# Raw-stream routers, and the experts' gather and sums as fp32r products of a rounded high part and a rest, in a two-block network on one Trainium2 core

## What is computed

```python
def rms_norm(x, g):
    xf = x.astype(F32)
    y = xf * lax.rsqrt(jnp.mean(xf * xf, axis=-1, keepdims=True) + EPS)
    return (y * g.astype(F32)).astype(x.dtype)

# per layer i:   hn = rms_norm(h, norm_ffn[i]);  h = h + hier_moe(hn, ...)
def hier_moe(h, wr_g, br_g, wr_e, br_e, w_gu, w_down):
    xf = h.reshape(T, D)
    p_group = softmax(xf @ wr_g + br_g)                 # 4 groups, top 1
    e_logits = xf @ wr_e + br_e                         # 32 experts, top 2 of the 8 in the group
    gates = pg * pv / jnp.sum(pv, axis=-1, keepdims=True)
    return grouped_experts(xf, expert_id, gates, w_gu, w_down)
# one expert on its tokens xb:  a, b = split(xb @ w_gu[e]);  (silu(a) * b) @ w_down[e]
# the rows are weighted by their gate and summed back to their tokens
```

## Time and profile before

| | |
|---|---|
| median of the runs | 2223.04 us |
| the profiled execution's own time | 2214.99 us |
| its span, first to last instruction | 2213.1 us |
| mean granted TensorE clock | 0.982 |
| busy: PE, DVE, ACT | 2089.7, 892.3, 669.1 us |
| HBM read | 600.73 MB |
| loop over the pairs, layer 0 | 951.2 to 1430.3 us |
| loop over the pairs, layer 1 | 1712.0 to 2189.3 us |

### The profile page before, as it was taken

One profiled execution on the slowest core, in us unless ns is written; L12 is line 12 of the kernel. 1 busy time (PEld: TensorE's weight loads), 2 busy tenths in 40 slices (PEclk: granted clock), 3 DMA queues, 4 the chain that ended last, 5 costly groups with the idle time before them and its releaser, 6 DMA issues.

```text
span 2213.1 us, 38037 instructions
## 1 busy us (share of the span) xinstructions
PE 2089.7 (94%) x15784; PEld 1525.4 (69%) x15785; DVE 892.3 (40%) x1468; ACT 669.1 (30%) x958; POOL 79.6 (4%) x118
## 2 busy tenths in 40 slices
PE   7997899998999998989999999999998999999998
PEld 5876899988999897844454444588987444444444
DVE  5866678745643544521111111165275111111112
ACT  3434464253652466311111111144342011111111
POOL 0100111101000200000000000000000000000000
PEclk9998999999999999999999999999999999999999
DMA  9731389803655251779999999535631899999993
GB/s 361 262 129 48 139 306 333 317 31 115 228 176 187 77 191 41 288 287 421 422 422 422 422 422 422 226 115 190 247 148 77 356 419 422 422 422 422 422 422 126
DMA packets 108084, 603.26 MB, mean 273 GB/s; under 512 B 10062, under 2 KB 10500, under 8 KB 58836
## 3 DMA queue, kind: packets, MB, share of 16 engines
q1 hardware_dynamic: 95872, 559.39, 63.9%
q0 software_dynamic: 11840, 42.34, 5.3%
q10 hardware_dynamic: 276, 0.13, 0.0%
HBM read 600.73 MB, written 1.05 MB: 272 GB/s over the span
## 4 chain that ended last, share of the span: by engine, by line
PE 88%; DVE 4%; ACT 4%; issue 2%; DMA 2%; SPq 0%; DVEq 0%; ACTq 0%
PE bank L939 20%; PE bank L951 10%; PE bank L551 10%; PE bank L552 10%; PE bank L553 10%; PE bank L923 6%; PE bank L970 5%; PE bank L581 4%; DMA dense_w<-in_w_in 1%; PE bank L561 1%; PE bank L562 1%; PE bank L560 1%; PE bank L594 1%; PE bank L631 1%; DVE work L1514 1%
## 5 line engine op out<-in xcount | busy, mean ns | idle before, releaser
L939 PE MATMUL bank<-expert_w,work 128*32 128x512 f32 (+1 forms) x4032 | 447.7, 594 | 24.0 <-issue 21.5
L939 PEld LDWEIGHTS bank<-expert_w,work 128*32 128x32 f32 (+1 forms) x4032 | 156.1, 110 | 314.2 <-issue 314.2
L434 DVE TENSOR_TENSOR w_low<-dense_w,w_high 128x2048 fp32r<-128x2048 f32 x112 | 256.1, 2290 | 221.5 <-ACT w_high L427 220.8
L427 ACT ACTIVATE w_high<-dense_w 128x2048 fp32r<-128x2048 f32 x120 | 228.6, 1911 | 312.1 <-DMA dense_w<-in_mlp_w 195.1
L951 PE MATMUL bank<-expert_w,work 128*32 128x512 f32 (+1 forms) x2016 | 226.4, 594 | 0.0
L2075 DVE TENSOR_TENSOR work<-work,bank 128x512 f32<-128x512 f32 x32 | 22.0, 688 | 400.3 <-ACT work L1404 400.3
L951 PEld LDWEIGHTS bank<-expert_w,work 128*32 128x32 f32 (+1 forms) x2016 | 63.5, 110 | 144.5 <-issue 144.5
L923 PEld LDWEIGHTS bank<-work 128*128 128x128 f32 x1088 | 133.1, 199 | 33.9 <-issue 33.8
L551 PE MATMUL bank<-u_pairs_mlp,w_high 128*128 128x256 f32 x512 | 145.2, 284 | 6.0 <-ACT u_pairs_mlp L1140 6.0
L923 PE MATMUL bank<-work 128*128 128x128 f32 x1088 | 139.2, 287 | 6.9 <-issue 6.9
L551 PE MATMUL bank<-hidden_pairs,w_high 128*128 128x256 f32 x512 | 144.9, 283 | 0.0
(11 more groups left out here) (379 smaller groups left out, 3620.8 us busy)
## 6 DMA issues: line engine op xcount, KB each, us to landing
expert_w<-in_expert_w_gu SPq DMA_DIRECT2D x256, 1024.0 KB, 13.1
expert_w<-in_expert_w_down SPq DMA_DIRECT2D x128, 1024.0 KB, 9.6
dense_w<-in_mlp_w SPq DMA_DIRECT2D x64, 1024.0 KB, 5.5
dense_w<-in_ret_w_in SPq DMA_DIRECT2D x24, 1024.0 KB, 5.4
u<-in_ada_w POOLq DMA_DIRECT2D x40, 512.0 KB, 6.2
work<-in_ada_w POOLq DMA_DIRECT2D x40, 512.0 KB, 6.9
dense_w<-in_fox_w_in SPq DMA_DIRECT2D x16, 1024.0 KB, 5.0
dense_w<-in_w_in SPq DMA_DIRECT2D x12, 1024.0 KB, 8.1
```

The lines of the kernel that those rows point to most:

```text
L427: nc.scalar.activation(HIGH_OF[at], dense_w[:, at % RING], ACT.Copy, scale=scale).then_inc(S("w_high_ready"), 1)
L434: ins = nc.vector.tensor_tensor(w_low[:, at % RING], dense_w[:, at % RING], high, ALU.subtract)
L939: last = mm(free[half][cols, :], rows[:, k, cols], pieces[:, k // 2, a, k % 2, half * 512:(half + 1) * 512], start=k == 0, stop=k == KT - 1)
```

## The change

- `moe_norm` goes. PE turns the raw `h` (4 banks of 4 transposes), and the router multiplies raw `h` by router weights that were scaled once by the norm's gain (a DVE product over both layers, ahead of the fox projections). The logits are multiplied by the token's reciprocal deviation when DVE reads them. ACT gets the squares' sums from the turned banks, and their root.
- The normed tokens are kept as `hn_high` (rounded, ACT) and `hn_low` (the rest, DVE), without the gain, which is applied when `xg` is copied. `pick` becomes fp32r. The gather is two fp32r products in place of each f32 one.
- y is kept as `y_high` and `y_low`; the slot's weight `slot_w`, summed from the turned `pick_w`, is applied at that copy, and `pickT` is zeros and ones. `add_up` is two fp32r products in place of each f32 one. The two halves of y are now each made by ACT and then by DVE.
- The eight warming products ahead of the first gather go, the order of `take_h` and of the weighing of the first pick is moved, and a fifth late load brings the gain, two values of each layout row in one run.

```diff
-                   ("moe_norm_0", 1), ("router_0", 2), ("hn_0", 4), ("combine_0", 4),
+                   ("hn_0", 4), ("router_0", 2), ("combine_0", 4),
...
+        hn_high = parts("hn_high", "work", 0, [TT, D])
+        hn_low = parts("hn_low", "u", 0, [TT, D])
...
+        y_high = parts("y_high", "work", 5632, [D])
+        y_low = parts("y_low", "work", 9728, [D])
+        pick = parts("pick", "work", 6656, [TT, P])
...
+        pickT = parts("pickT", "work", 7680, [TT * P])
+        slot_w = small[:, 92:93]
...
             def experts(l):
-                rms_norm(f"moe_norm_{l}")
+                out = TILES["ret_out" if l else "fox_out"]
+                for q in range(4):
+                    t = TILES[f"hn_{l}"] + q
+                    tt, half = q % 2, q // 2
+                    open_bank(pe, t)
+                    for n in range(4):
+                        k = 4 * half + n
+                        wait_evac(pe, out + k)
+                        last = nc.tensor.transpose(bank(t)[:, n * P:(n + 1) * P], h[:, k, tt * P:(tt + 1) * P], ident)
+                    last.then_inc(tile_ready, 1)
...
-                        last = mm(bank(t)[:, tt * NR:(tt + 1) * NR], u[:, k, tt * P:(tt + 1) * P], router_w[:, l, k, :],
+                        last = mm(bank(t)[:, tt * NR:(tt + 1) * NR], h[:, k, tt * P:(tt + 1) * P], router_w[:, l, k, :],
...
+                take_h(0)
+                take_h(1)
...
+                take_h(2)
+                take_h(3)
...
                         for tt in range(TT):
-                            last = mm(free[2 + half][:, (k % 4) * P:(k % 4 + 1) * P], every_other(hn_tok[:, tt], k),
-                                      source[:, tt, :], start=tt == 0, stop=tt == TT - 1)
+                            for x in (hn_high, hn_low):
+                                last = mm(free[2 + half][:, (k % 4) * P:(k % 4 + 1) * P], every_other(x[:, tt], k), source[:, tt, :],
+                                          start=tt == 0 and x is hn_high, stop=tt == TT - 1 and x is hn_low)
...
                     for k in range(KT):
-                        last = mm(total[k // 2][:, (k % 2) * SEQ:(k % 2 + 1) * SEQ], y_sb[:, k * P:(k + 1) * P],
-                                  pick_wT.rearrange("p t n -> p (t n)"), start=False, stop=False)
+                        for y in (y_high, y_low):
+                            last = mm(total[k // 2][:, (k % 2) * SEQ:(k % 2 + 1) * SEQ], y[:, k * P:(k + 1) * P], pickT,
+                                      start=False, stop=False)
...
-                for _ in range(WARM):
-                    mm(free[3][:, 0:SEQ], ident, K("rope_cos"), start=True, stop=True)
...
             def experts(l):
-                rms_squares(f"moe_norm_{l}", added("ret_out" if l else "fox_out"))
+                eps = const[:, CONSTS["eps"][0]:CONSTS["eps"][0] + 1]
+                fn(small[:, 90:91], eps, ACT.Sqrt)
+                for q in range(4):
+                    wait_tile(act, TILES[f"hn_{l}"] + q)
+                    at = 80 + 2 * (q // 2) + q % 2
+                    fn(part(wk, 4096 + 512 * q, 512), bank(TILES[f"hn_{l}"] + q)[:, :], ACT.Square,
+                       accum_out=small[:, at:at + 1]).then_inc(S("hn_moments"), 1)
+                act.wait_ge(S("hn_stats"), 2 * l + 1)
+                fn(small[:, 86:88], small[:, 84:86], ACT.Sqrt, scale=1.0 / D, bias=eps).then_inc(S("hn_moments"), 1)
+                act.wait_ge(S("hn_stats"), 2 * l + 2)
+                for q in range(4):
+                    fn(hn_high[:, q % 2, q // 2 * 512:(q // 2 + 1) * 512], bank(TILES[f"hn_{l}"] + q)[:, :], ACT.Copy,
+                       scale=small[:, 88 + q % 2:89 + q % 2]).then_inc(S("hn_high"), 1)
...
                 def take_xg(rows, done):
-                    fn(rows[:, 0:4, :], free[2][:, :].rearrange("p (k n) -> p k n", k=4), ACT.Copy).then_inc(done, 1)
+                    for k in range(4):
+                        last = fn(rows[:, k, :], free[2][:, k * P:(k + 1) * P], ACT.Copy, scale=ffn_gain[:, KT * l + k:KT * l + k + 1])
+                    last.then_inc(done, 1)
...
                 def take_y(done):
-                    fn(y_sb[:, 0:512], free[2][:, :], ACT.Copy).then_inc(done, 1)
+                    for half in range(2):
+                        fn(y_high[:, half * 512:(half + 1) * 512], free[2 + half][:, :], ACT.Copy, scale=slot_w).then_inc(done, 1)
...
+            ffn_rows = vec[:, P + VEC2["ffn"]:P + VEC2["ffn"] + DEPTH * KT].unsqueeze(2).broadcast_to([P, DEPTH * KT, NR])
+            routers = router_w[:, :, :, :].rearrange("p l k n -> p (l k) n")
+            V.tensor_tensor(routers, routers, ffn_rows, ALU.mult).then_inc(S("cum_ready"), 1)
...
+                dve.wait_ge(S("hn_moments"), 5 * l + 4)
+                V.tensor_tensor(small[:, 84:86], small[:, 80:82], small[:, 82:84], ALU.add).then_inc(S("hn_stats"), 1)
+                V.tensor_scalar(y_low, const[:, 0:D], 0.0, None, ALU.mult).then_inc(S("y_dve"), 1)
+                V.tensor_scalar(pickT, const[:, 0:SEQ], 0.0, None, ALU.mult).then_inc(S("pick_wT_ready"), 1)
+                dve.wait_ge(S("hn_moments"), 5 * l + 5)
+                V.reciprocal(small[:, 88:90], small[:, 86:88]).then_inc(S("hn_stats"), 1)
...
+                def low_of_hn(q):
+                    t, at = TILES[f"hn_{l}"] + q, slice(q // 2 * 512, (q // 2 + 1) * 512)
+                    dve.wait_ge(S("hn_high"), 4 * l + q + 1)
+                    evac(V.scalar_tensor_tensor(hn_low[:, q % 2, at], bank(t)[:, :], small[:, 88 + q % 2:89 + q % 2],
+                                                hn_high[:, q % 2, at].bitcast(f32), ALU.mult, ALU.subtract), t)
+                low_of_hn(0)
+                low_of_hn(1)
...
+                for tt in range(TT):
+                    std = small[:, 88 + tt:89 + tt]
+                    V.scalar_tensor_tensor(pad8[:, tt, 0:GROUPS], logits[:, tt, 0:GROUPS], std, bias[:, 0:GROUPS], ALU.mult, ALU.add)
+                    last = V.scalar_tensor_tensor(lg[:, tt, :], logits[:, tt, :], std, bias, ALU.mult, ALU.add)
...
+                low_of_hn(2)
+                low_of_hn(3)
...
                 def take_pick_wT(done):
-                    V.tensor_copy(pick_wT, free[1][:, 0:SEQ].rearrange("p (t n) -> p t n", t=TT)).then_inc(done, 1)
-
-                def take_y(done):
-                    V.tensor_copy(y_sb[:, 512:1024], free[3][:, :]).then_inc(done, 1)
+                    V.tensor_reduce(slot_w, free[1][:, 0:SEQ], AX.X, ALU.add)
+                    V.tensor_scalar(pickT, free[1][:, 0:SEQ], 0.0, None, ALU.is_gt).then_inc(done, 1)
+
+                def take_y(made, at, done):
+                    for half in range(2):
+                        dve.wait_ge(made, at + half + 1)
+                        eight = slice(half * 512, (half + 1) * 512)
+                        last = V.scalar_tensor_tensor(y_low[:, eight], free[2 + half][:, :], slot_w, y_high[:, eight].bitcast(f32),
+                                                      ALU.mult, ALU.subtract)
+                    last.then_inc(done, 1)
...
+            pool.dma_start(ffn_gain[:, :].rearrange("p (k r) -> p k r", r=2),
+                           A["vec2"][VEC2["ffn"]:VEC2["ffn"] + DEPTH * KT, :].rearrange("n q -> (n q)").rearrange(
+                               "(k m r) -> m k r", m=P, r=2)).then_inc(S("in_late"), 16)
```

More of the change, by code:

```diff
@@ L257, in build @@
         hidT = part(wk, 5120, 4, P)
-        y_sb = part(wk, 5632, D)
-        pick = part(wk, 6656, TT, P)
+        y_high = parts("y_high", "work", 5632, [D])
+        y_low = parts("y_low", "work", 9728, [D])
+        pick = parts("pick", "work", 6656, [TT, P])
         pick_w = part(wk, 6912, TT, P)
-        pick_more = part(wk, 7168, TT, P)
+        pick_more = parts("pick_more", "work", 7168, [TT, P])
         pick_w_more = part(wk, 7424, TT, P)
-        pick_wT = part(wk, 7680, TT, P)
+        pickT = parts("pickT", "work", 7680, [TT * P])
+        slot_w = small[:, 92:93]
         is_first = part(wk, 7936, TT, P)
@@ L295, in build @@
         rt = sb("rt", [P, 40])
+        ffn_gain = sb("ffn_gain", [P, DEPTH * KT])
         rel = sb("rel", [P, 2, TT])
@@ L869, in experts, with take_h @@
             def experts(l):
-                rms_norm(f"moe_norm_{l}")
+                out = TILES["ret_out" if l else "fox_out"]
[8 more added lines that the diff above has]
+                    last.then_inc(tile_ready, 1)
                 t = TILES[f"router_{l}"]
                 open_bank(pe, t)
-                pe.wait_ge(S("in_late"), 16 * 4)
+                pe.wait_ge(S("cum_ready"), 3)
                 for k in range(KT):
-                    pe.wait_ge(*out_of(f"moe_norm_{l}", k + 1))
                     for tt in range(TT):
-                        last = mm(bank(t)[:, tt * NR:(tt + 1) * NR], u[:, k, tt * P:(tt + 1) * P], router_w[:, l, k, :],
+                        last = mm(bank(t)[:, tt * NR:(tt + 1) * NR], h[:, k, tt * P:(tt + 1) * P], router_w[:, l, k, :],
```

(34 more changed lines are left out.)

52 lines of the change are left out of this document (22 added, 30 removed).

## The result

The changed kernel takes 2208.73 us (median of 20 runs, 2196.74 to 2224.51), the kernel before 2220.42 (20 runs, 2212.16 to 2228.44): a ratio of 0.995 with a 95% interval from 0.9933 to 0.9967, so 11.7 us less. The forecast was 34.6 less. The sign was right and the time lies in the range, but two thirds of the gain are missing, and the runs spread over 28 us where those of before spread over 16.

The account below looks back on a forecast made before the run. Prediction: PE's pair (29.55 us) hides slightly slower loads (29.82) by a lead, so loads would bind a faster PE; 2 x (13.4 + 0.4 + 3.5) = 34.6 less, from 2223.04 to 2188.4, range a little under 2166 to 2222.

Parts of the forecast that it names:

- loop, layer 0: Loop over layer 0's expert pairs: 13.4 us less, from 1.55 in pair 0, the lead 10.3 and 1.55 behind the last piece.
- Then 32 x 0.124 = 3.97 and nothing changes: Gather in each pair: 32 rounded products at 0.124 us each take 3.97, as the f32 gather does.
- The forecast of the loops' bound: Both expert loops: PE's pair falls to 28.00 us, below the loads' 29.82, so PE later waits for gate/up pieces.
- a lead that is used up: Expert loop: the last gate/up load lands 10.3 us before its read; this shrinks 1.82 a pair, gone after some eight pairs.
- the loads keep up: Rival, expert loops: loads do not bind, PE's whole saving counts, 57.4 us less, 2166; chance 0.06.
- The second way to the last piece's landing: Layer 0's loop: from 983.2, 84 double loads at 422 GB/s take 417.4 us, so the last gate/up piece lands at 1400.6.
- Ahead of the loop: Stretch before each layer's expert loop: the new order saves 3.5 us a layer, with ends of 5 less and 5 more.
- I take 1.2 for that: Ahead of each loop: 1.2 us allowed for the lower clock, as a gather at half clock took 6.15 instead of 3.97.
- Behind the last pair: After each loop's last pair: copies 1.4 us more, add_up 1.9 instead of 3.69, so 0.4 less.
- A narrow fp32r product is dear: Rival, gather: under 256 columns rounded products stream four times, 0.216 us each, 6.91 a gather, 2265 in all; chance 0.20.
- The stretch ahead grows: Rival, ahead of the loops: ACT and DVE alternate, PE arrives at half clock, 5 us more a layer, 2205; chance 0.12.

Follow-up runs that it names:

- gather in f32, warmed: Changed kernel with gather back in f32 products and eight warming products put back ahead of each layer's first gather: 2185.86 us, 0.985 to the kernel before.
- half of add_up: Changed kernel with gather in f32 and add_up's products with y's rest left out: 2191.75 us, 0.9874 to the kernel before.
- short loads: Expert loads of pairs 1 to 15 bring 1536 of 2048 columns: 2229.59 us in the changed kernel, 2158.61 us with its gather in f32.
- warmed kernel: Changed kernel, gather still rounded, with eight warming products put back ahead of each layer's first gather: 2195.4 us, 0.9896 to the kernel before.

## Why the prediction was wrong, point by point

Profiled executions, differences to before in us. A stretch ahead runs from the end of the output projection to the loop.

| term | forecast | after, 4 stops | gather in f32, warmed |
|---|---|---|---|
| ahead, layer 0 | -3.5 | -3.0 | -5.9 |
| loop, layer 0 | -13.4 | +11.4 | -12.0 |
| ahead, layer 1 | -3.5 | -6.5 | -9.2 |
| loop, layer 1 | -13.4 | -3.3 | -8.4 |
| behind, and between | -0.8 | +3.2 | +1.8 |
| up to fox_out's end | 0 | +2.5 | +3.4 |
| span | -34.6 | +4.3 | -30.2 |

- **The step that failed is the gather's**: "Then 32 x 0.124 = 3.97 and nothing changes". The price in a steady pair was right (3.92). But behind a stop of 3.3 us or more the rounded gather takes 6.2 to 7.1 in every profile and does not get the clock back: the four turns of the hidden rows behind it take 0.89 where they take 0.55 in steady pairs, and the rounded add_up up to 3.41 instead of 1.91. The f32 gather took 5.4 to 6.2 and brought the clock back, with turns of 0.47 as in its steady pairs. Two pairs of kernels differ in the gather (and in DVE's four rests that go with it, worth some 2 us), each set against the kernel before on its chip: 12.3 above against 10.2 below, so 22.6 lost (add_up in f32), and 11.7 below against 29.2 below, so 17.5 lost (add_up rounded). Of the 17.5, the half clock alone makes some 11: with one stop in the loop, a loop lasts 472.1 to 473.9 with the rounded gather (seven loops of the changed kernel) and 467.1 to 468.9 with the f32 one (three loops), 5.3 less on average. Some 3 lie ahead of the loops. The rest, some 4, is left for further stops, and that the format brings these is not shown. I read the stop of pair 0 in the trace of before and used it as a price of half clock for the first gather; I did not ask what the new gather would do behind it.
- **The forecast of the loops' bound was right.** Period 28.0, a lead that is used up, then 29.83; half of add_up gives nothing, and short loads give it all. Even the rival "the loads keep up" has its number there: 2166 by the sum, 2158.6 measured with short loads. With the gather in f32 layer 0's loop gains 12.0 of 13.4. From the loads' restart in pair 0 (979.4, by the DMA share of 0.19 in 977 to 980) to the last piece's landing it takes 419.0 (979.4 to 1398.4) where I had 417.4, 1.6 more, which is about the rest. One reading was off: I put the restart of the kernel before at 983.2, but its load is issued at 983.50, and the share of 0.46 in 983.2 to 986 puts the full rate at 984.7. The second way to the last piece's landing then gives 1402.1 and not 1400.6, still close to 1401.3.
- With one stop a loop the changed kernel's loops last 473.7 and 472.2 (span 2192.6), a gain of 5.4 and 5.1. In layer 0 the load that restarts the queue is issued 35.0 behind the loop's start (981.92 less 946.91) instead of 32.3 (983.50 less 951.19): pair 0 did not save 1.55 but lost 2.7 at half clock, while the load queue was dry.
- **Ahead of the loop** 3.5 a layer was forecast; the trace of after gives 3.0 and 6.5, of which 4.14 is the stop at layer 1's entry that didn't come again there: luck, as nothing in the forecast asked for it. The term "I take 1.2 for that" was too small: the first gather (6.72 at 942.27) took 3.0 more than in the warmed kernel, and the first project (16.69), already in the loop, 2.8 more. This is the failed step once more, at another place: with the f32 gather and no warming the first project takes 13.94. Warming alone, with the gather left in rounded parts, brings 10.4. With the f32 gather and warmed, the stretch gains 5.9 and 9.2.
- **Behind the last pair** I had 0.4 less. The timeline of after (start us, us, engine, line, operation, [idle before]), against the earlier trace rows:

```profile
1441.30 1.26 ACT L1437 ACTIVATE y_high<-bank,small 128x512 fp32r<-128x512 f32 x2 [8.64 <-PE bank L961]
1442.02 1.41 DVE L2122 SCALAR_TENSOR_TENSOR y_low<-bank,small,y_high 128x512 fp32r<-128x512 f32 x2 [7.08 <-ACT y_high L1437]
...
1443.53 0.36 PE L981 MATMUL bank<-pickT,y_high 128*128 128x256 f32 x1 [2.38 <-ACT y_high L1437]
...
1445.06 0.41 PE L981 MATMUL bank<-pickT,y_high 128*128 128x256 f32 x1
```

The copies take 2.3 (two of ACT, two of DVE) where I had 2.2, but add_up falls to half clock on the way, where its records take 0.41 and not 0.28: 3.0 instead of 1.9. Copies and add_up together take 5.3 where they took 4.5: 0.8 more and not 0.4 less.

- **Rivals.** "A narrow fp32r product is dear" falls (3.92, not 6.91). "The stretch ahead grows" came nearest in time, 2205, and it named the half clock at the loop; but the stretches themselves shrank, and the loss lies inside the loop. No rival held what decided.

What stays open is what makes a stop recur. Of eleven profiles with the rounded gather, three had stops in pairs behind the first (one of them with short loads, in ten pairs running); of six with the f32 gather, one had a single one. These are too few to tie the count to the gather's format, and the two long executions with short loads and the f32 gather have no trace. The address of the code moves a stop, but equal code had two and four of them. I have no mechanism that gives the count.

## What to carry to other kernels

A product that is cheaper or equal in a steady stream must also be priced behind a pause: look in the trace for every place where the engine stands still, and ask what the first products behind it do with the clock, and what runs dry meanwhile. Where loads are the bound, PE's savings are worth only the lead and what lies ahead of and behind the loads, but its losses count as soon as they hold back the slots. When the runs of a kernel spread by ten or twenty us, take several profiles before explaining one of them.

## What had not been expected of the hardware

- PE stops for 3.3 to 4.9 us in a long loop that it has just entered, and again in later pairs in some executions, with a packet of 16.4 thousand bytes on the instruction queue, and taking out or adding code that is never run moves the stop (1.38 and 2.50 with less; 4.64 and 2.41 with more, the first at the loop entry).
- 32 rounded products of 128 columns run for 7.06 us at a granted clock of 0.50 and it does not rise, while 32 f32 records of the same width behind such a stop take 5.53 and the next ones are at full clock. In steady pairs the two cost 3.92 and 3.97.
- Of equal executions of one kernel some have one stop a loop and some three, which makes 8.4 to 8.9 us for each further one in the loop: spans from 2192.6 to 2217.4 for the changed kernel.
